# Scaling the attention probabilities on GpSimd, and logits kept negated with their minimum

## The reference

```python
lg_own = jnp.einsum("bhcd,bhld->bhcl", qc, k_own, preferred_element_type=jnp.float32) * scale
lg_own = lg_own - slope_f[None, :, None, None] * dist_own[None, None]
lg_own = jnp.where((dist_own >= 0)[None, None], lg_own, NEG)
logits = jnp.concatenate([lg_sel.reshape(B, H, Q_CHUNK, n_sel * L), lg_own], axis=-1)
w = jax.nn.softmax(logits, axis=-1).astype(vb.dtype)
```

## Time and profile before

| | |
|---|---|
| median of 3 runs | 665.81 us (665.48 to 665.88) |
| profiled execution | 666.83 us, span 664.9 us |
| TensorE matmul busy | 654.8 us (98%) |
| VectorE busy | 371.5 us (56%) |
| ScalarE busy | 287.2 us (43%) |
| GpSimd busy | 319.0 us (48%) |
| mean DMA rate | 98 GB/s |

### The profile page before, as it was taken

How to read it: one execution, slowest core, us unless ns; L and a number is a source line. 1 busy time by engine, 2 the same in 40 slices (tenths; PEclk the granted TensorE clock), 3 DMA queues, 4 the chain that set the end, 5 groups by cost and what they waited for, 6 DMA issues and landing times.

```text
span 664.9 us, 8664 instructions
## 1 busy us (share of the span) xinstructions
PE 654.8 (98%) x2978; PEld 542.9 (82%) x2978; DVE 371.5 (56%) x518; ACT 287.2 (43%) x432; POOL 319.0 (48%) x232
## 2 busy tenths in 40 slices
PE   7999999999999999999999999999999999999997
PEld 5888888887888888888888888888888888888886
DVE  5682689889867677655555555555522222222464
ACT  5657653656656444433333433333422222223521
POOL 6664343703114647655555555555555554444430
PEclk9999999999999999999999999999999999999999
DMA  8633221210041314222223223322222222222211
GB/s 318 256 112 111 96 95 64 95 33 1 0 159 54 115 54 158 95 95 95 95 95 101 98 100 99 105 97 95 95 96 96 95 95 95 95 95 96 79 63 48
DMA packets 20181, 65.39 MB, mean 98 GB/s; under 512 B 2368, under 2 KB 3008, under 8 KB 20160
## 3 DMA queue, kind: packets, MB, share of 16 engines
q1 hardware_dynamic: 19584, 64.57, 28.6%
q10 hardware_dynamic: 576, 0.53, 0.2%
HBM read 62.99 MB, written 2.10 MB: 98 GB/s over the span
## 4 chain that ended last, share of the span: by engine, by line
PE 92%; DVE 3%; ACT 2%; issue 1%; DMA 1%; ACTq 0%; DVEq 0%
PE bank L958 29%; PE bank L959 29%; PE bank L960 29%; PE bank L996 1%; ACT prob L475 1%; DVE prob L789 1%; PE bank L999 1%; PE bank L1004 1%; PE bank L1106 1%; DVE prob L801 1%; DMA raw<-in_weights 1%; PE bank L1092 1%; PE bank L1054 1%; DVE prTlo L837 0%; ACT prThi L489 0%
## 5 line engine op out<-in xcount | busy, mean ns | idle before, releaser
L298 POOL TENSOR_TENSOR wlo<-raw,whi 128x512 fp32r<-128x512 f32 x106 | 142.5, 1344 | 315.9 <-ACT whi L331 315.9
L331 ACT ACTIVATE whi<-raw 128x1024 fp32r<-128x1024 f32 x106 | 111.8, 1057 | 228.0 <-PE bank L960 227.9
L958 PE MATMUL bank<-uhi,whi 128*128 128x512 f32 (+1 forms) x496 | 192.5, 388 | 0.0
L960 PE MATMUL bank<-uhi,wlo 128*128 128x512 f32 (+1 forms) x496 | 191.3, 386 | 0.0
L959 PE MATMUL bank<-ulo,whi 128*128 128x512 f32 (+1 forms) x496 | 191.3, 386 | 0.0
L299 POOL TENSOR_TENSOR wlo<-raw,whi 128x512 fp32r<-128x512 f32 x106 | 164.9, 1556 | 0.0
L958 PEld LDWEIGHTS bank<-uhi,whi 128*128 128x128 f32 x496 | 93.2, 188 | 19.5 <-issue 0.7
L959 PEld LDWEIGHTS bank<-ulo,whi 128*128 128x128 f32 x496 | 93.2, 188 | 19.4 <-issue 0.7
L960 PEld LDWEIGHTS bank<-uhi,wlo 128*128 128x128 f32 x496 | 93.2, 188 | 18.6
L892 DVE SCALAR_TENSOR_TENSOR tmp<-tmp,vec 128x511 f32<-128x511 f32 (+1 forms) x48 | 64.8, 1349 | 27.9 <-ACT tmp L537 24.8
L958 PE MATMUL bank<-acthi,whi 128*128 128x512 f32 x192 | 74.7, 389 | 0.0
(11 more groups left out here) (184 smaller groups left out, 834.8 us busy)
## 6 DMA issues: line engine op xcount, KB each, us to landing
raw<-in_weights SPq DMA_DIRECT2D x106, 512.0 KB, 3.3
res<-in_x_t SPq DMA_DIRECT2D x8, 256.0 KB, 7.3
xtok<-in_x SPq DMA_DIRECT2D x4, 512.0 KB, 9.6
out<-fin SPq DMA_DIRECT2D x7, 256.0 KB, 2.0
raw<-in_weights SPq DMA_DIRECT2D x6, 256.0 KB, 8.0
gw<-in_gates SPq DMA_DIRECT2D x1, 512.0 KB, 12.7
ptok<-in_p_t SPq DMA_DIRECT2D x1, 512.0 KB, 3.4
raw<-in_weights ACTq DMA_DIRECT2D x2, 128.0 KB, 5.5
```

The costliest lines, as they stand in the source:

```text
L298: nc.gpsimd.tensor_tensor(wlo[s][:, 0:CW // 2], raw[s][:, 0:CW // 2], whi[s][:, 0:CW // 2].bitcast(F32), ALU.subtract)
L331: nc.scalar.activation(whi[s][:, :], raw[s][:, :], ACT.Copy).then_inc(w_hi, 1)
L958: mm(o, ahi, bhi, start=start, stop=False)
L960: return mm(o, alo, bhi, start=False, stop=stop)
```

## The change

VectorE no longer scales the probabilities. `normalise(h)` moves to GpSimd, which waits for the reciprocals (`rinv_ok`) and does the four scalings; VectorE keeps only the reciprocal, in `sums(h)`. GpSimd's loop over the chunks is cut in two, and between the halves stand the eight `normalise` and, written out, the four `lo_part` that fall into the heads.

The logits are computed with the negated slope and reduced by minimum, so the buffer holds minus the logits and `sm` holds minus the maximum. The exponential then takes scale -1 and this value as its bias. The instruction that negated the maxima (L793) and its semaphore go; each exponential waits for its own part of the logits and not for all four.

```diff
@@ GpSimd @@
-            with pool.Fori(2, N_CHUNKS // RING) as i:
+            with pool.Fori(2, C_OA // RING) as i:
+                for s in range(RING):
+                    lo_part(s + i * RING, s)
+
+            def normalise(h):
+
+                pool.wait_ge(rinv_ok, h + 1)
+                for i, _, _ in SCORES:
+                    v = prob[h % 2][:, S_OFF[i]:S_OFF[i] + (i + 1) * P]
+                    nc.gpsimd.tensor_scalar(v, v, sm[:, h % 2, 12 + i:13 + i], None, ALU.mult).then_inc(prob_ok, 1)
+
+            normalise(0)
+            for h in range(HEADS):
+                if h + 1 < HEADS:
+                    normalise(h + 1)
+                if h in (1, 2, 4, 6):
+                    lo_part(C_OA + h // 2, h // 2)
+            with pool.Fori(C_UP // RING, N_CHUNKS // RING) as i:
                 for s in range(RING):
                     lo_part(s + i * RING, s)
@@ ScalarE @@
-                act.wait_ge(nmax_ok, h + 1)
-                for i, _, _ in SCORES:
+                for n, (i, _, _) in enumerate(SCORES):
                     v = prob[h % 2][:, S_OFF[i]:S_OFF[i] + (i + 1) * P]
-                    nc.scalar.activation(v, v, ACT.Exp, bias=sm[:, h % 2, 4 + i:5 + i],
+                    act.wait_ge(logit_ok, 4 * h + n + 1)
+                    nc.scalar.activation(v, v, ACT.Exp, bias=sm[:, h % 2, i:i + 1], scale=-1.0,
                                          accum_out=sm[:, h % 2, 8 + i:9 + i]).then_inc(exp_ok, 1)
@@ VectorE @@
                     V.tensor_tensor_reduce(prob[h % 2][:, S_OFF[i]:S_OFF[i] + w], bank[b][:, c0:c0 + w],
-                                           dist[:, (TT - 1 - i) * P:T], slope(h), 3.0 * NEG, ALU.add, ALU.max,
+                                           dist[:, (TT - 1 - i) * P:T], -slope(h), -3.0 * NEG, ALU.add, ALU.min,
                                            sm[:, h % 2, i:i + 1]).then_inc(logit_ok, 1)
-                dve.wait_ge(logit_ok, 4 * (h + 1))
-                V.tensor_scalar(sm[:, h % 2, 4:8], sm[:, h % 2, 0:4], -1.0, None, ALU.mult).then_inc(nmax_ok, 1)
-
-            def normalise(h):
+
+            def sums(h):
                 dve.wait_ge(exp_ok, 4 * (h + 1))
                 V.reciprocal(sm[:, h % 2, 12:16], sm[:, h % 2, 8:12]).then_inc(rinv_ok, 1)
-                dve.wait_ge(rinv_ok, h + 1)
-                for i, _, _ in SCORES:
-                    v = prob[h % 2][:, S_OFF[i]:S_OFF[i] + (i + 1) * P]
-                    V.tensor_scalar(v, v, sm[:, h % 2, 12 + i:13 + i], None, ALU.mult).then_inc(prob_ok, 1)
```

More of the change, by code:

```diff
@@ L200, in build @@
         v_hi, v_lo, qg_ok = sem("v_hi"), sem("v_lo"), sem("qg_ok")
-        s_done, logit_ok, nmax_ok, exp_ok, rinv_ok, prob_ok = (
-            sem(n) for n in ("s_done", "logit_ok", "nmax_ok", "exp_ok", "rinv_ok", "prob_ok"))
+        s_done, logit_ok, exp_ok, rinv_ok, prob_ok = (
+            sem(n) for n in ("s_done", "logit_ok", "exp_ok", "rinv_ok", "prob_ok"))
         pt_done, prT_hi, prT_lo, pv_done = (sem(n) for n in ("pt_done", "prT_hi", "prT_lo", "pv_done"))
@@ L822, in _ @@
             add_lru(0)
-            normalise(0)
+            sums(0)
             logits(1)
@@ L841, in _ @@
                 if h + 1 < HEADS:
-                    normalise(h + 1)
+                    sums(h + 1)
                 if h + 2 < HEADS:
```

## The result

The changed kernel takes 679.91 us (median of four runs, 677.64 to 680.50), the kernel before 665.85 us beside it: a ratio of 1.0203 with an interval of 1.0184 to 1.0222. It is slower by 2.0%, where 0.31% faster was forecast and 668.0 us was the upper end of the range.

A forecast was written before the change was run, and what follows sets the result against it. TensorE, busy 654.8 of 664.9 us, bounds the kernel; removing 2.09 us of stalls in the heads takes the profiled execution from 666.83 to 664.74, the median, 1.02 lower, to 663.72. Forecast 663.7 us, range 663.0 to 668.0.

The forecast's parts named there:

- GpSimd's part: New path in each head: reciprocal, four scalings on GpSimd, next turn; claimed 6.52 us, so no stall left.
- X: Time of the four scalings on GpSimd in each head: taken as 1.81 us, upper bound 3.47.
- the first sign of being wrong: In every head, the turns wait for GpSimd; this would mean four scalings of over 2.6 us.
- the prediction's own rival: GpSimd becomes the late engine in the heads: scalings 3.47 us, every head 8.18, total 670.8 us; chance 0.14.
- The Trainium skill's sentence: Scalings on GpSimd: read as a doubling, it would give 2.56 us for the four, a gain of 1.38, 664.4 us.
- The rest of the path: From turn to turn in the heads, all besides the four scalings: 4.71 us.
- GpSimd takes the place of VectorE as the late one: In the heads, four scalings of 3.47 us make every head 8.18 us: 670.8 us in all; chance 0.14.
- The stalls to give back: TensorE's lost time in the heads, between turns 2 and 7: 0.66 + 0.60 + 0.42 + 0.41 = 2.09 us.
- the negated logits cost nothing: VectorE's logits in the heads: same instruction with another operation, minus the slope and minimum at no cost.
- GpSimd's remainders behind the scalings: GpSimd's `lo_part` in the heads, at turn + 6.5 to + 9.2 us, claimed to block nobody.
- nothing after the heads takes the change back: After 200 us TensorE has no gap, so the gain reaches the end; rival, absorbed by later wait: 665.8 us, 0.04.

The follow-up runs named there:

- the copies: The changed kernel with a plain copy in place of each scaling on GpSimd, all waits kept: 663.18 us beside 665.92, ratio 0.9961.

## Why the prediction was wrong

- **GpSimd's part, the value of X: the step that failed.** I put the four scalings between 1.81 and 3.47 us and took 1.81, "the nearest row is the select on `dist`". They take 4.27 us, beyond the upper bound. The wait of every turn for GpSimd is the first sign of being wrong that the prediction named. The trace of before had no row of this form, and both ends were drawn from other instructions as if the number of tensors read set the rate. It does not: the same instruction takes 0.70 or 1.57 us for 512 columns by whether its second operation is given; why, stays open. With X = 4.27 the prediction's own rival, carried to that value, gives turn 7 at 136.16 + 4.27 + 0.05 + 7 x 8.98 = 203.3 us; it came at 203.96. That this is so near is in part luck: the path was 0.13 us too long in each of seven heads, and the 1.5 us of the clock were missing.
- **The Trainium skill's sentence.** GPSIMD Engine Reference, Engine selection, calls one-input work on GpSimd roughly line rate. I had sided with it. The copy and the two-operation form come near it, with 1.65 and 2.06 us for the four against VectorE's 1.28. The one-operation form that the change uses does not: 4.27 us, 3.3 times VectorE's time.
- **The clock: not in the prediction.** I read the full clock in all slices and took it as given. The gap before each turn, 1.5 us and before turn 7 2.2 us, brought it down in two heads of the profiled execution and at turn 7: 3.2 us.
- **The rest of the path.** I had 4.71 us plus X; it is 4.58. Doing without the negation and with separate waits of the exponentials, which I priced at nothing, brings 0.14 us: the exponentials had waited for the negation.
- **The rival with the sign right.** "GpSimd takes the place of VectorE as the late one" is what happened, with its mechanism and place, but it had a chance of 0.14 and 670.8 us. The rest of the way to 679.91 is the size of X, 4.27 and not 3.47, for some 6 us, and the clock.
- **What was right.** The stalls to give back (2.09; 2.22 with the copies), that they came from scalings stretched beside GpSimd, that up to turn 6 they end if X is under 2.6 (the limit that the measured path gives is 7.33 - 4.58 = 2.75), that the negated logits cost nothing, that GpSimd's remainders behind the scalings block nobody, and that nothing after the heads takes the change back: the kernel with copies comes to 663.18 us where the forecast was 663.7.

## What to carry to other kernels

Before work goes to another engine, time the very form of the instruction there, with its operands and its operations; a neighbour in the trace with as many inputs is no bound, here it was off by a factor of more than two. Two numbers decide such a move: the slack of the receiving path (2.75 us here up to turn 6) and the price of the work there. And where two engines overlap and one is stretched, moving the other's work out of the way can be enough: a few lines on GpSimd gave 2.4 us (interval 1.5 to 3.5), about the 2.1 us that the change was after.

## What was unexpected of the hardware

- On GpSimd a scaling with one operation takes 1.49 us (constant) or 1.57 us (per-partition factor) for 512 columns in fp32; with a second operation written out, even times 1.0 or plus 0.0, 0.62 us with constants, 0.70 us with one factor, 0.77 us with two. In the heads the same holds: 1568 ns against 695.
- A product of two tensors on GpSimd took 1.04 us for 512 columns, less than the scaling with one operation.
- An idle gap of TensorE of about 1.5 us between stretches of dense work was followed by a granted clock below full, 0.65 over the next 4 us, in some heads and not in others; the gap filled with twelve transposes was not.
- One of VectorE's scalings, of 256 columns, took 1.38 us and not 0.35 when GpSimd had begun a subtraction just before it, and it ended 0.15 us after that one. In the changed kernel VectorE's additions and logits of 512 columns took 0.65 to 0.69 us beside GpSimd's scalings, as before.
